# Expert blocks computed ahead during the scatter: from the turned table, split by GpSimd, with 14 blocks instead of 12 and no TensorE drain

## The reference, cut to what matters

```python
def peer(h, w_query, sub_keys, expert_u, expert_v):
    ...
    best_s, best_pos = lax.top_k(cand_s, PEER_TOPK)
    idx = jnp.take_along_axis(cand_i, best_pos, axis=-1)
    gates = jax.nn.softmax(best_s, axis=-1).astype(h.dtype)
    ...
        u = jnp.take(expert_u, idx_blk, axis=0)
        act = jax.nn.gelu(jnp.einsum('thkd,td->thk', u, h_blk))
        vv = jnp.take(expert_v, idx_blk, axis=0)
        return jnp.einsum('thk,thkd->td', g_blk * act, vv)
```

## Time and profile before

| | us |
|---|---|
| median of 3 runs | 2951.24 |
| lowest, highest | 2950.57, 2951.73 |
| span of the profiled execution | 2947.2 |
| retrieve, end of it and opening of the scatter | up to 1077.9 |
| scatter, first to last TensorE copy | 1077.9 to 1281.8 |
| expert loop, first step of the v products to the end | 1318.3 to 2947.2 |

### The profile page before, as it was taken

The page is one execution under the profiler, slowest core; times in us unless marked ns, Lnnn a source line. Parts: engine busy times, 40 slices in busy tenths (PEclk is TensorE's granted clock), DMA queues, the critical chain, the costliest instruction groups (busy, mean ns, idle before and its releaser), DMA issues.

```text
span 2947.2 us, 48734 instructions
## 1 busy us (share of the span) xinstructions
PE 2850.5 (97%) x16467; PEld 2523.1 (86%) x16467; DVE 2427.2 (82%) x4619; ACT 1119.2 (38%) x2218; POOL 1226.7 (42%) x987
## 2 busy tenths in 40 slices
PE   6999999999999989999999999999999999999997
PEld 4888888878888889988888898899889888888896
DVE  6446666675589999979999989889989899999898
ACT  6121444533456655542333333333332333333233
POOL 0001000010178820026666656555555566655564
PEclk9999999999999999999999999999999999999999
DMA  7425444244211128799999999999999999999999
GB/s 264 160 96 192 135 119 119 95 142 152 101 55 39 36 77 276 244 341 371 357 361 370 369 339 352 335 332 358 343 337 343 357 366 364 366 362 350 356 364 283
DMA packets 348742, 764.96 MB, mean 260 GB/s; under 512 B 21340, under 2 KB 177592, under 8 KB 343232
## 3 DMA queue, kind: packets, MB, share of 16 engines
q0 software_dynamic: 117296, 423.15, 38.4%
q1 hardware_dynamic: 223600, 336.18, 33.8%
q10 hardware_dynamic: 7712, 3.93, 0.4%
HBM read 688.82 MB, written 74.36 MB: 259 GB/s over the span
## 4 chain that ended last, share of the span: by engine, by line
PE 38%; DVE 13%; DMA 6%; issue 6%; PEld 5%; POOL 2%; DVEq 1%; ACT 1%; POOLq 0%; PEldq 0%; ACTq 0%; SPq 0%
PE psum L2655 17%; PE psum L2648 17%; DMA ex_v_row<-in_expert_v,ex_row 4%; PEld psum L1783 3%; DVE ex_u_row L2904 3%; DVE acc L2916 3%; PE psum L203 2%; PEld psum L2336 2%; DMA w_dram<-sc_w 1%; DVE rt_rest L2080 1%; DVE ex_v_lo L2899 1%; DVE h_lo L2895 1%; DVE rt_top_f L2079 1%; DVE rt_top_f L2088 1%; DMA ex_u_row<-in_expert_u,ex_row 1%
## 5 line engine op out<-in xcount | busy, mean ns | idle before, releaser
L2606 POOL DMA_INDIRECT ex_u_row<-in_expert_u,ex_row x384 | 420.3, 1095 | 732.3 <-DVE ex_dot L2904 411.4
L2606 POOL DMA_INDIRECT ex_v_row<-in_expert_v,ex_row x384 | 533.8, 1390 | 158.5 <-issue 109.7
L2916 DVE SCALAR_TENSOR_TENSOR acc<-ex_v_row,ex_coef,acc 128x1024 f32<-128x1024 f32 x381 | 489.3, 1284 | 45.8 <-DMA ex_v_row<-in_expert_v,ex_row 45.3
L2904 DVE CUSTOM_DVE_ANT_0 ex_u_row<-ex_u_row,h_rows 128x1024 f32<-128x1024 f32 x384 | 466.8, 1216 | 7.1 <-DMA ex_u_row<-in_expert_u,ex_row 6.8
L2655 PE MATMUL psum<-ex_v_hi,ex_c_lo 128*128 128x512 f32 x1260 | 341.7, 393 | 12.4 <-DVE ex_v_lo L2899 12.3
L2655 PE MATMUL psum<-ex_v_lo,ex_c_hi 128*128 128x512 f32 x1260 | 339.2, 391 | 0.0
L2655 PE MATMUL psum<-ex_v_hi,ex_c_hi 128*128 128x512 f32 x1260 | 338.7, 391 | 0.0
L2648 PE MATMUL psum<-h_hi,h_lo 128*128 128x320 f32 x1696 | 285.1, 310 | 10.0 <-DVE acc L2978 8.5
L2655 PEld LDWEIGHTS psum<-ex_v_hi,ex_c_lo 128*128 128x128 f32 x1260 | 234.4, 188 | 61.9 <-issue 15.7
L2648 PE MATMUL psum<-h_lo,h_hi 128*128 128x320 f32 x1696 | 283.4, 310 | 0.0
L2648 PE MATMUL psum<-h_hi 128*128 128x320 f32 x1696 | 283.3, 310 | 0.0
(11 more groups left out here) (386 smaller groups left out, 5279.8 us busy)
## 6 DMA issues: line engine op xcount, KB each, us to landing
ex_vn<-in_expert_v SPq DMA_DIRECT2D x64, 1024.0 KB, 7.3
ex_un<-in_expert_u_t SPq DMA_DIRECT2D x42, 1024.0 KB, 8.5
ex_w<-w_dram SPq DMA_DIRECT2D x64, 640.0 KB, 9.9
w_dram<-sc_w SPq DMA_DIRECT2D x9, 4096.0 KB, 14.9
gm_wm<-in_w_mod SPq DMA_DIRECT2D x14, 1024.0 KB, 5.5
pj_raw<-in_w_in SPq DMA_DIRECT2D x11, 1024.0 KB, 7.3
ex_un<-in_expert_u_t SPq DMA_DIRECT2D x22, 512.0 KB, 7.5
pr_wm<-in_w_mod SPq DMA_DIRECT2D x8, 1024.0 KB, 14.2
```

Of the source, the lines that this page charges most:

```text
L2606: nc.gpsimd.indirect_dma_start(to[:], None, all_rows, bass.IndirectOffsetOnAxis(row[s][:, col:col + 1], 0)).then_inc(done, 16)
L2904: nc.vector.tensor_tensor_reduce(out=u_row[k % 3][:], in0=u_row[k % 3][:], in1=h_rows[:, k % 3, :], scale=1.0, scalar=0.0, op0=ALU.mult, o ...
L2916: nc.vector.scalar_tensor_tensor(out=to, in0=v_row[k % 3][:], scalar=coef[:, k:k + 1], in1=to, op0=ALU.mult, op1=ALU.add).then_inc(row_use ...
```

## The change

Scatter no longer turns raw rows on TensorE. Its blocks are loaded from the turned table as those of the retrieve stage are (`fetch`), ScalarE makes the high part with one instruction of 128 x 1024 (`raise_columns`), and GpSimd makes the low part (`lower_columns`; the first block's in `prepare`, the other 13 in the new `Scatter.gpsimd`). `turn`, `leave`, `upper` and `lower` are gone, and with them the constant `minus`.

EXTRA goes from 6 to 8, so JOBS from 12 to 14 and the blocks ahead from 22 to 24; LATE falls from 9 to 7. The halves are placed by `unit_at`: 28 halves in three of every four groups, the last one in group 36. TensorE's drain behind each group is gone; who waited for `placed` now waits for `copied`, the semaphore of the copies themselves.

```diff
-    EXTRA = 6
+    EXTRA = 8
...
     def load(self, sp, n, m):
-        sp.wait_ge(self.turned, (n - self.HEADS) * 2 + 2)
-        sp.dma_start(self.un[m][:], self.u_rows[:, bass.ds(self.block(n), 1), :].rearrange("j a d -> j (a d)")).then_inc(self.un_in[m], 16)
+        sp.wait_ge(self.lowered, n - 1)
+        self.fetch(sp, n, m)
...
+    def fetch(self, sp, n, m, to=None):
+        step, e = divmod(self.block(n), 2)
+        to = self.un[m] if to is None else to
+        sp.dma_start(to[:].rearrange("p k x -> p (k x)"), self.u_columns[step, :, e, :]).then_inc(self.un_in[m], 16)
...
     def hide(self, pe, n, m, half):
-        if n < self.HEADS:
-            pe.wait_ge(self.lowered, n + 1)
-        else:
-            pe.wait_ge(self.lo_out, (n - self.HEADS) * 2 + 4)
+        pe.wait_ge(self.lowered, n + 1)
...
@@ Scatter.prepare
+            ahead.lower_columns(pool, nc.gpsimd, *self.job(0))
...
-            ahead.turn(pe, n, m, n // 2)
...
-            ahead.upper(act, *self.job(0))
+            ahead.raise_columns(act, *self.job(0))
...
-            ahead.lower(act, *self.job(0))
...
+    def unit_at(self, g):
+
+        u = 3 * (g // 4) + g % 4
+        return divmod(u, 2) if g % 4 < 3 and u < 2 * self.JOBS else None
...
@@ Scatter.vector
-                dve.wait_ge(self.placed, g - 1)
+                dve.wait_ge(self.copied, 4 * (g - 1))
...
@@ Scatter.tensor
-        ahead.leave(pe, *self.job(0))
...
-            pe.drain().then_inc(self.placed, 1)
-            k = g // 3
-            if k < self.JOBS and g % 3 < 2:
-                ahead.hide(pe, *self.job(k), g % 3)
-            if k + 1 < self.JOBS and g % 3 >= 1:
-                n, m = self.job(k + 1)
-                if g % 3 == 1:
-                    ahead.turn(pe, n, m, n // 2)
-                else:
-                    ahead.leave(pe, n, m)
+            unit = self.unit_at(g)
+            if unit:
+                ahead.hide(pe, *self.job(unit[0]), unit[1])
...
@@ Scatter.scalar
-            k = g // 3
-            if k < self.JOBS and g % 3 < 2:
-                ahead.gelu(act, self.job(k)[0], g % 3)
-            if k + 1 < self.JOBS and g % 3 >= 1:
-                (ahead.upper if g % 3 == 1 else ahead.lower)(act, *self.job(k + 1))
+            unit = self.unit_at(g)
+            if unit:
+                k, half = unit
+                ahead.gelu(act, self.job(k)[0], half)
+                if half == 0 and k + 1 < self.JOBS:
+                    ahead.raise_columns(act, *self.job(k + 1))
...
+    def gpsimd(self, pool):
+
+        for k in range(1, self.JOBS):
+            self.ahead.lower_columns(pool, self.nc.gpsimd, *self.job(k))
...
@@ Scatter.sync
+                if half == 1 and k + 3 < self.JOBS:
+                    ahead.load(sp, *self.job(k + 3))
...
@@ experts, gpsimd
-        pool.wait_ge(scatter.placed, scatter.GROUPS - 1)
+        scatter.gpsimd(pool)
+        pool.wait_ge(scatter.copied, 4 * (scatter.GROUPS - 1))
```

More of the change, by code:

```diff
@@ L1694, in __init__ @@
         self.u_columns = expert_u_t
[L1695 removed]
         self.dram = core.dram("ahead_dram", [self.BLOCKS, P, 2, HD])
         self.un_in, self.stored = core.sems("ah_un_in", 2, True), core.sems("ah_stored", 2, True)
[L1698 to L1700 removed]
+        self.raised, self.lowered, self.hidden, self.gelued = (
+            core.sem(f"ah_{n}", True) for n in ("raised", "lowered", "hidden", "gelued"))
     def place_heads(self):
@@ L1753, in store @@
         sp.dma_start(self.dram[bass.ds(n, 1), :, half, :].rearrange("a e t -> e (a t)"), self.g[half][:]).then_inc(self.stored[half], 16)
[L1755 to L1762, removed]
-                                             start=k == 0, stop=k == 3, is_transpose=True, skip_group_check=True)
-            last.then_inc(self.turned, 1)
-    def leave(self, pe, n, m):
-        for q in range(2):
-            pe.wait_ge(self.hi_out, (n - self.HEADS) * 2 + (q + 1))
-            self.nc.tensor.matmul(self.turn_bank[q].rearrange("p (k n) -> p k n", k=4), self.t.minus[:], self.ut(self.ut_hi, m, q),
-                                  start=False, stop=True, skip_group_check=True).then_inc(self.left, 1)
     def hide(self, pe, n, m, half):
-        if n < self.HEADS:
-            pe.wait_ge(self.lowered, n + 1)
-        else:
-            pe.wait_ge(self.lo_out, (n - self.HEADS) * 2 + 4)
+        pe.wait_ge(self.lowered, n + 1)
         pe.wait_ge(self.gelued, n * 2 + (half + 1))
@@ L2048, in _ @@
         chunk(0)
-        nc.scalar.activation(t.minus[:], t.ident[:], ACT.Copy, scale=-1.0)
         chunk(1)
@@ L2396, in sync @@
         for g in range(self.GROUPS):
-            tile, k = g // self.NG, g // 3
-            if k < self.JOBS and g % 3 < 2:
-                ahead.store(sp, self.job(k)[0], g % 3)
-            if k + 3 < self.JOBS and g % 3 == 1:
-                ahead.load(sp, *self.job(k + 3))
+            tile, unit = g // self.NG, self.unit_at(g)
+            if unit:
+                k, half = unit
+                ahead.store(sp, self.job(k)[0], half)
+                if half == 1 and k + 3 < self.JOBS:
+                    ahead.load(sp, *self.job(k + 3))
             if g % self.NG == self.NG - 1 and tile < self.TILES - 1:
@@ L2629, in _ @@
             gather(u_all, u_row[k], 2, k, u_row_in[k])
-        pool.wait_ge(scatter.placed, scatter.GROUPS)
+        pool.wait_ge(scatter.copied, 4 * scatter.GROUPS)
         with pool.Fori(0, NSTEP // 2 - 1) as i:
```

36 lines of the change are left out of this document (8 added, 28 removed).

## The result

The changed kernel takes 2966.95 us (median of 4 runs, 2962.60 to 2971.16) against 2950.9 us for the kernel before in the same session. The ratio is 1.0059, 95% interval [1.0044, 1.0073]. Measured a second time in another session it is 2961.35 us (6 runs) at 1.0043 [1.0031, 1.0055]. So the change costs 13 to 16 us, 0.4 to 0.6%: slower, with both intervals clear of 1. I had forecast 2955 us and no measurable change as the likeliest. Both medians lie inside the stated range of 2937 to 2968, but above the 2950 to 2961 of my own case, and on the slower side that I held less likely than no change. One execution of all that follow, one of the twelve of the last experiment, took 3744.03 us at a granted clock of 0.71 and is left out of its median and ratio.

The account below looks back on a forecast made before the run. TensorE was taken to bound the expert loop and, closely, the scatter, where VectorE would set the pace after the change. Span 2947.2 + 17 - 13 = 2951.2, plus 4.0 to the median: 2955 us, range 2937 to 2968.

Parts of the forecast that it names:

- my own case: Whole kernel: VectorE held up by GpSimd's subtractions, the loop shorter; 2955 us, range 2950 to 2961, chance 0.62.
- the loop's gain of 13.0 us: Expert loop: periods 7 and 8 become late ones, 98.1 instead of 104.60 us each; bounds -13.2 and 0.
- smaller terms at nothing: ScalarE's evictions, the loads, SP's wait for `lowered`, GpSimd's first gathers and TensorE's waits for the low part: no cost.
- VectorE's floor of 4.71 us a group: Scatter: VectorE's own work is unchanged, 4.71 us a group, 18.8 for four, just above TensorE's 18.3.
- the gain of the drain: Scatter: without TensorE's drain, if VectorE's floor were all, the last copies start at 1265 instead of 1279.80, 15 us earlier.
- the opening: Scatter's opening: GpSimd's first subtraction delays a VectorE sum, and so the first group, by 2.2 us; bounds 0 and 2.4.
- the mechanism that decides: Scatter: each of 13 GpSimd subtractions shuts out VectorE's two-input instructions, 2.3 us each, 29.9 in all; bounds 0 and 2.40 each.
- The rivals without the exclusion: Scatter: 16-bit VectorE instructions run on beside GpSimd, so VectorE's floor counts; 2923 us, chance 0.10.
- with half of it: Scatter: GpSimd works in VectorE's gaps or the opening escapes; 13 x 1.2 instead of 29.9 us, 2940 us, chance 0.10.
- the last one: Expert loop: it gives nothing, as another engine pays for the halves taken from TensorE; 2968 us, chance 0.05.
- late periods too tight: Expert loop: late-landing rows stall two late periods, so 2 x 5.2 us are lost; 2966 us, chance 0.13.
- scatter and opening: From the opening to the scatter's last copies: group 39's copies start at 1296.7 instead of 1279.80, +17 us (15 to 19).

Follow-up runs that it names:

- the last experiment: The kernel before without TensorE's drain and with 13 instead of 12 blocks in the scatter, made by transposes: 2943.17 us, ratio 0.9983 to the kernel before.

## Why the prediction was wrong

The mechanism was right and the sum was not: the loop's gain of 13.0 us was about twice what it gives, and smaller terms at nothing were not nothing.

**What held.** The limit of the loop and of the scatter, VectorE's floor of 4.71 us a group, the gain of the drain (within the -15 that I gave "if that were all"; alone it measured -14 to -15, though on 12 blocks made by transposes), the opening (+2.2 said, 2.0 at the row and 2.6 to 2.9 to the first copies), and the mechanism that decides: GpSimd's subtraction shuts out VectorE's instructions for its whole length. I had put 2.3 us on each; it is 2.08, so 27.0 instead of 29.9. Part of that is a slip: from my own premises (VectorE would have started 0.08 before its last end, GpSimd begins 0.13 before that end and lets VectorE in 0.13 before its own) the sum is 2.40 - 0.13 - 0.13 + 0.08 = 2.22, not 2.34, and 2.2 is what the instructions that ran without a break show. The rest is the four that stood in a wait of VectorE. The 2.9 us too many hid as much of the terms that I left out, which is luck. The rivals without the exclusion, or with half of it, are refuted by the rows above, and the loop does give something, against the last one.

**The step that failed most: the loop's -13.0 us.** I took both new late periods at 98.1. Period 7 is; period 8 takes 103.7 here, 104.4 in the second profile, and 102.8 to 104.6 in every other form with 14 blocks but one (101.9, without the low part). In both profiles of the changed kernel it is one row of v, 5.1 and 4.6 us late for VectorE. This is my own rival "late periods too tight", to which I gave 0.13, come true for one of the two; I had reckoned with one such period in six as with chance. It is no chance: period 13 takes over 100 us in every profile, and period 8 does it as soon as it is late. Measured, the two periods give 7.5 us in the profiled pair and 6.6 in the second profile instead of 13.0. Over all profiles with 14 blocks against all with 12 the loop is 1618.1 against 1625.2, so 7; the four with 12 blocks alone spread from 1620.7 to 1628.9.

**A term that I left out: the last half.** I had worked out that TensorE carries halves behind groups 36 to 38 and that the two engines arrive together, but not that ScalarE's rounding of the loop's first block waits for the half behind group 36, and VectorE's split for that. VectorE is a chain with no air here, so the 2.4 us count: with 12 blocks the wait is 0.3 us and the scatter shorter by more than its two subtractions. The half behind group 37 in the last experiment makes 7.5 of them.

**Terms at nothing that were not.** After waits for VectorE TensorE falls into the slow clock (from the first copies to the first product a granted 0.50, which is 1.2 GHz, for 3.4 or 6.8 us at six places, against two before). Its copies then come up to 4 us behind, and VectorE waits for them 2.6 us in all. The 27.0 us of the subtractions, the last half's 2.4 and these 2.6, less the 13.1 of waits for the drain that are gone, are 18.9; the scatter is 18.4 us longer in the first profile and 18.9 in the second, instead of my 14.7. The stretch behind it grew by 4.1 us in the first pair and by 2.8 in the second profile. Over the profiles of 14 blocks it is 39.0 to 43.2, of 12 blocks 38.5 to 40.7; how much of that is the change's, and through what, stays open.

**In sum,** first and second profile: scatter and opening +21.0 and +21.8 (forecast +17), behind it +4.1 and +2.8 (0), loop -8.8 and -10.7 (-13), and +1.9 and -0.4 ahead of the change (0), which is the spread between executions. Scatter, the stretch behind it and the loop all err the same way. My own case had 2950 to 2961 and the measurement says 2961 to 2967.

**Still open:** why the row that period 8 and period 13 wait for comes late there and not in others. The loading of other periods is as high (a DMA share of 0.95 to 0.98) and they pass. What the trace adds is that GpSimd issues this row late. Its gathers in period 8 of the changed kernel, and VectorE's instruction that waits for the second:

```profile
2240.59 1.66 POOL L2567 DMA_INDIRECT ex_u_row<-in_expert_u,ex_row  x1 [2.63 <-DVE ex_dot L2865]
2242.55 1.56 POOL L2567 DMA_INDIRECT ex_v_row<-in_expert_v,ex_row  x1 [0.30 <-issue]
```

```profile
2252.48 1.28 DVE L2877 SCALAR_TENSOR_TENSOR acc<-ex_v_row,ex_coef,acc 128x1024 f32<-128x1024 f32 x1 [5.07 <-DMA ex_v_row<-in_expert_v,ex_row]
```

The row is issued 55.7 us behind the start of period 8; in every profile of this document, the kernel before included, it is 55.7 there and 52.6 to 52.8 in periods 7, 9 to 12 and 14, and wherever period 8 is a late one VectorE waits 4.1 to 5.4 us at this row. It takes 9.9 us to land, about what a row issued at that time in period 7 takes (9.7). In the kernel before, where period 8 is an ordinary one, the row is issued as late and lands in 6.1 us, so nothing waits. Period 13 has such a late issue near its start (6.6 us instead of about 3.5; 6.2 in one profile). So these are fixed places, not chance; what delays the issue there no run shows.

## What to carry to other kernels

Before work is given to an idle GpSimd, look at what VectorE does beside it: if VectorE sets the pace with instructions of two SBUF inputs, each GpSimd instruction that reads SBUF costs VectorE most of GpSimd's working time (2.08 of 2.40 us here), and VectorE doing it itself can be cheaper (1.14 against 2.08 us here). A change of several parts should be priced and run part by part: here one line, the drain, was worth 14 to 15 us, and the rest of it cost about twice that and made the line worth nothing. Where work is taken out of equal periods, a period that has a stall ready behind it gives little back (1.0 us of 6.5 in period 8), so count the gain by periods that have shown the shorter time, not by the mean of the clean ones.

## What I had not expected of the hardware

A GpSimd fill of 128 x 1024 fp32 (0.95 us, 14 times) runs beside VectorE's two-input instructions at no cost to either, while a copy of the same size costs VectorE 0.8 us and a subtraction 2.1 us. GpSimd doesn't wait for VectorE's drain to get in: it takes its turn at the end of any instruction, so that four pieces of a subtraction and four instructions of VectorE alternate one by one, and the whole costs the same (24.8 against 27.0 us). In the changed kernel that wait makes GpSimd's own rows 2.4 to 3.4 us long. And GpSimd issues one row gather 3.0 us late in the same period of the loop in every profile; VectorE then waits 4.1 to 5.4 us where that period is a late one, and under 3 us where it is not.
